# The order of key tiles, gates and the first merge stage ahead of attention A in layer 0

## The reference, cut to what matters

```python
qa = apply_rope(rms_norm(br['qa'], lw['q_norm']), cos, sin)      # 8 heads
ka = apply_rope(rms_norm(br['ka'], lw['k_norm']), cos, sin)      # 2 key/value heads
a_out = dense_gqa(qa, jnp.concatenate([ka, ka_ctx], axis=1),
                  jnp.concatenate([br['va'], va_ctx], axis=1), N_KV_A)
ya = (a_out * jax.nn.silu(br['ga'])) @ lw['w_proj_a']
g_a, g_b, g_c = jnp.split(jax.nn.sigmoid(h @ lw['w_gate'] + lw['b_gate']), N_BRANCH, axis=-1)
```

## Time and profile before

| | us |
|---|---|
| median of 3 runs | 1404.5 (1404.39 to 1404.72) |
| the profiled execution, its own time | 1406.98 |
| its span in the trace | 1405.2 |
| PE busy | 1361.3 (97%) |
| DVE busy | 768.6 (55%) |
| POOL busy | 692.9 (49%) |
| ACT busy | 624.2 (44%) |

### The profile page before, as it was taken

The page is one execution under the profiler, slowest core; times in us unless marked ns, Lnnn a source line. Parts: engine busy times, 40 slices in busy tenths (PEclk is TensorE's granted clock), DMA queues, the critical chain, the costliest instruction groups (busy, mean ns, idle before and its releaser), DMA issues.

```text
span 1405.2 us, 22465 instructions
## 1 busy us (share of the span) xinstructions
PE 1361.3 (97%) x8654; PEld 1259.1 (90%) x8654; DVE 768.6 (55%) x1605; ACT 624.2 (44%) x1298; POOL 692.9 (49%) x500
## 2 busy tenths in 40 slices
PE   7999999999999999999999999999999999999997
PEld 5898989899888899999888988998989989999985
DVE  5656773263884511656685577722468715036557
ACT  4336876334765221223264478851367633222230
POOL 3455565234565354355653566642256554445453
PEclk9999999999999999999999999999999999999999
DMA  9412101222112344354421211012121042225421
GB/s 362 137 61 65 31 31 33 74 79 68 39 46 68 127 151 150 112 204 136 135 97 47 87 61 31 31 46 79 61 63 43 31 136 68 68 76 195 131 80 75
DMA packets 36762, 126.94 MB, mean 90 GB/s; under 512 B 5040, under 2 KB 5680, under 8 KB 36656
## 3 DMA queue, kind: packets, MB, share of 16 engines
q1 hardware_dynamic: 29952, 108.54, 23.1%
q10 hardware_dynamic: 6704, 16.97, 3.4%
HBM read 119.73 MB, written 5.77 MB: 89 GB/s over the span
## 4 chain that ended last, share of the span: by engine, by line
PE 85%; DVE 5%; POOL 4%; ACT 2%; issue 2%; DVEq 0%; POOLq 0%; ACTq 0%
PE ps L949 50%; PE ps L897 6%; PE ps L899 6%; PE ps L898 6%; PE ps L1096 4%; PE ps L1086 3%; PE ps L1088 2%; PE ps L1107 2%; PE ps L1108 2%; POOL with_eps L1778 1%; POOL w_lo L1794 1%; DVE x L1759 1%; PE ps L966 1%; POOL p_f_a L1820 1%; PE ps L1115 1%
## 5 line engine op out<-in xcount | busy, mean ns | idle before, releaser
L1794 POOL TENSOR_TENSOR w_lo<-raw,w_hi 128x1024 fp32r<-128x1024 f32 x148 | 360.2, 2440 | 270.6 <-ACT w_hi L1151 184.9
L949 PE MATMUL ps<-h_hi,w_hi 128*128 128x320 f32 x1280 | 295.6, 312 | 8.7 <-DVE g_c L1699 4.6
L949 PE MATMUL ps<-h_hi,w_lo 128*128 128x320 f32 x1280 | 291.9, 309 | 0.0
L949 PE MATMUL ps<-h_lo,w_hi 128*128 128x320 f32 x1280 | 291.5, 309 | 0.0
L949 PEld LDWEIGHTS ps<-h_hi,w_hi 128*128 128x128 f32 x1280 | 218.1, 188 | 25.5 <-DVE g_c L1699 6.0
L1151 ACT ACTIVATE w_hi<-raw 128x1024 fp32r<-128x1024 f32 x148 | 154.1, 1055 | 148.3 <-DMA raw<-in_weights 70.6
L949 PEld LDWEIGHTS ps<-h_lo,w_hi 128*128 128x128 f32 x1280 | 215.2, 188 | 1.6
L949 PEld LDWEIGHTS ps<-h_hi,w_lo 128*128 128x128 f32 x1280 | 215.0, 188 | 1.8
L897 PE MATMUL ps<-w_hi,h_hi 128*128 128x512 f32 (+1 forms) x360 | 129.8, 361 | 1.2 <-POOL w_lo L1794 1.0
L899 PE MATMUL ps<-w_hi,h_lo 128*128 128x512 f32 (+1 forms) x360 | 128.3, 357 | 0.0
L898 PE MATMUL ps<-w_lo,h_hi 128*128 128x512 f32 (+1 forms) x360 | 128.0, 356 | 0.0
(11 more groups left out here) (184 smaller groups left out, 2630.3 us busy)
## 6 DMA issues: line engine op xcount, KB each, us to landing
raw<-in_weights SPq DMA_DIRECT2D x190, 512.0 KB, 3.4
raw_more<-in_weights SPq DMA_DIRECT2D x10, 512.0 KB, 10.4
x<-in_x_sample ACTq DMA_DIRECT2D x6, 512.0 KB, 9.8
x_mid<-x ACTq DMA_DIRECT2D x5, 512.0 KB, 2.6
x<-x_mid ACTq DMA_DIRECT2D x5, 512.0 KB, 6.7
y_sample<-x SPq DMA_DIRECT2D x3, 512.0 KB, 2.6
pack<-in_pack ACTq DMA_DIRECT2D x2, 528.0 KB, 6.7
x<-in_x_sample SPq DMA_DIRECT2D x2, 512.0 KB, 5.2
```

What stands on the lines that cost most here:

```text
L949: last = pe.matmul(ps[:, s + half, 0:HALF], w[:, u % RING, cols], acts[:, k, half * HALF:(half + 1) * HALF], start=k == 0 and part == 0, s ...
L1794: did(pool.tensor_tensor(w_lo[:, n % RING, :], raw_tile(r), w_hi[:, n % RING, :], ALU.subtract), w_ready)
```

## The change

In layer 0 the list between the key and value product and attention A is written anew. Before, the order is: key and value tiles 0 and 1; gate 2; queries 4; tile 2; zeros; gate 3; exponential table; queries 0; key tile 0; tile 3; key tile 1; tile 4; key tile 2; merge stage 0 whole; key tile 3; cached keys; 2 warm matmuls; key tile 4.

After, it is: tile 0; cached keys; tile 1; zeros; gate 2; queries 4; key tiles 0 and 1; tiles 2 and 3; gate 3; key tile 2; tile 4; exponential table; queries 0; key tile 3; first half of merge stage 0; key tile 4; second half. The two warm matmuls are left out.

The state outputs move from the event of the cached tile to that of key tile 1, in both layers and for both branches.

```diff
     if l == 0:
         kvm = mm("kv_a")
+        first_z = ("z", l, 0, 0)
+        first_z_of = chunks(first_z, 2)
         out.extend([qs[1], qs[2], *whole(gate("a", 0)), queries[1], qs[3], *whole(gate("a", 1)), queries[2], qs[4],
-                    kvm[0], queries[3], qs[0], kvm[1], kv[0], kv[1], *whole(gate("a", 2)), queries[4], kv[2],
-                    ("zeros", l), *whole(gate("a", 3)), ("table_of_exp", l, "a"), queries[0], keys[0], kv[3], keys[1], kv[4], keys[2], *whole(("z", l, 0, 0)), ("pool", 0, 1, 2, 3, 4, 5),
-                    keys[3], keys[5], ("warm", 2, 4), keys[4]])
+                    kvm[0], queries[3], qs[0], kvm[1], kv[0], keys[5], kv[1], ("zeros", l), *whole(gate("a", 2)), queries[4],
+                    keys[0], keys[1], kv[2], kv[3], *whole(gate("a", 3)), keys[2], kv[4], ("table_of_exp", l, "a"), queries[0],
+                    keys[3], first_z_of[0], keys[4], first_z_of[1], first_z, ("pool", 0, 1, 2, 3, 4, 5)])
...
                         if t == CACHE:
                             did(act.activation(vv[:, CACHE, :, 0, :], cache_v[:, "ab".index(br), :, :], ACT.Copy), v_hi_made)
+                        if t == 1:
                             act.wait_ge(staged, NO[("in", l, "kv_" + br, 0)] + 1)
                             load(state_out, outs[f"state_{br}_k"][0, l], k_st[:, 0, :, 0, :])
                             load(state_out, outs[f"state_{br}_v"][0, l].rearrange("p h d -> p (h d)"), v_st[:, :])
```

## The result

The changed kernel took 1407.68 us (median of 11 executions, 1405.21 to 1408.75), the kernel before 1404.39 (11 executions, 1403.49 to 1405.84). The two medians are 3.3 us apart. The ratio estimated from all these executions is 1.0019, that is 2.7 us, with a 95% interval of 1.0011 to 1.0027: 1.5 to 3.8 us slower, small but clear of 1. All executions of this study together give medians of 1406.4 (24 of the changed kernel) and 1404.5 (76 of before): **1.9 us slower**. The forecast was 0.6 us slower, 1405.1 us, and the range ended at 1407.4: the first median lies 0.3 us above that end, the second and the pooled one within the range.

A forecast was written before the change was run, and what follows sets the result against it. PE was taken to bound the kernel (85% of the chain that ended last). The terms +4.2 + 1.5 - 3.6 - 1.5 + 0 gave +0.6 us on the median of 1404.5: 1405.1 us, range 1403.2 to 1407.4.

The forecast's parts named there:

- Step 1: Ahead of the third gate: PE waits for DVE to drain the cached keys' bank; gate starts 4.2 us later.
- Step 2: At the third gate: the clock falls within or after the stall, costing 1.5 us (bounds 0.4 and 3.0).
- My sign for a wrong size: Around the third gate: the low clock lasting beyond one stretch would make the prediction's size wrong.
- Step 3: From the third gate's Silu to the scores: 3.6 us less than 21.4, mainly from waits that go.
- Step 4: At the first scores: with the waits gone the clock stays up, 1.5 us less (bounds 0 and 1.5).
- Step 5: State outputs moved on ACT in four lead-ins: no effect, 0, bounds -0.5 and +0.5 us for all four.
- A: Rival: no stall at the third gate, sum -4.9, 1399.6 us; chance 0.08.
- B: Rival: the clock dip at the scores stays, sum +2.1, 1406.6 us; chance 0.12.
- C: Rival: the clock stays low through the third gate, sum +6.1, 1410.6 us; chance 0.07.
- D: Rival: waits return at key tile 4 or first probabilities, 1 to 2 us lost, 1406 to 1407 us; chance 0.10.

The follow-up runs named there:

- e1: The changed kernel with layer 0's cached keys transposed into PSUM bank 0 instead of bank 5: 1399.97 us against 1404.76 before.
- e6: The changed kernel with the cached keys moved between the third and fourth gate, no bank fixed by hand: 1405.52 us against 1404.16 before.
- e7: The changed kernel, unedited, profiled a second time to look at its clock: 1405.81 us.
- e8: The changed kernel, unedited, profiled a third time to look at its clock: 1405.1 us.
- e9: The changed kernel, unedited, timed again against the kernel before: median 1406.14 us against 1404.49, ratio 1.0011.
- e10: The changed kernel with 8 instead of 3 warm matmuls in PE's wait at 24 us: 1405.66 us against 1404.49 before.
- e2: The changed kernel with 16 unneeded warm matmuls between the cached transposes and the third gate: 1403.96 us, ratio to before 0.9993.
- e5: The kernel before with more warm matmuls (7 and 8 instead of 2 and 2) in its two waits ahead of the scores: 1403.36 us against 1404.16.
- e11: The changed kernel with the cached keys in bank 0 and 8 instead of 3 warm matmuls at 24 us: 1399.76 us against 1404.49 before.
- e3: The kernel before with only the state outputs moved to key tile 1, both layers and branches: 1404.75 us against 1404.76.
- e4: The kernel before with only the cached keys moved ahead of the third gate, state outputs with key tile 1: 1409.1 us against 1404.76.

## Why the prediction was right, and where its sizes were off

**Step 1, the stall: right, in place, cause and size.** 4.0 us from the transposes to the gate against 4.2, and 3.62 idle against 3.9 (just under the 3.7 to 4.1 that I had named as its sign). The short duration of the last instruction held: 0.28 us. e1 shows that the bank is the cause and not the place in the list, and in e6 the wait follows the bank to the next gate.

**Step 2, the clock on the third gate: right that it falls, too small.** I took the 1.5 us of another dip. The profiles show 9.47 - 7.04 = 2.4 at first, then 2.5 and 1.4 (e7, e8), and 1.6 in e9 and in e10. The gate in e10 (102.98 - 94.30 = 8.68):

```profile
94.30 0.80 PE L951 MATMUL ps<-h_hi,w_hi 128*128 128x320 f32 x2 [3.61 <-DVE vv L1621]
...
102.98 0.60 PE L1065 MATMUL ps<-ident_r,q_st 128*128 128x128 f32 x4
```

As times, the median of e10 (stall empty) less the usual time of e2 (stall filled; 7 of its 11 executions lie at 1403.7 to 1404.0) gives 1405.66 - 1403.93 = 1.7. All lie between my bounds of 0.4 and 3.0. My sign for a wrong size, a low clock beyond one stretch, did come in the first profile: about 4.9 us of the gate's work ran at the low level (twice the 2.43 lost), against 3.3 us in the dip at the scores.

**Step 3, the lead from gate to scores: right.** 122.98 less the Silu at 105.45 (gate end at 105.25 plus the 0.2 of the earlier trace rows) is 17.5, by the trace's record of that start; 17.8 was worked out, 21.4 was before. Most of the 0.3 too much is the warm matmuls, which I took at their duration of 0.6; the scores start 0.37 behind them (122.61 to 122.98). The steps kept apart by a tenth did fit: key tile 4 came at 117.97, and no wait stands there. Where no execution has a low clock the kernels are cleanest to compare: e2 is at 1403.9 (7 of 11), and e5, the kernel before without its dip, at 1403.1 to 1403.4 (6 of 11), say 1403.2: +0.7 for a sum of +4.2 - 3.6 = +0.6. By the traces it is +0.3: 28.9 us from the cached transposes to the first scores in e2 (90.27 to 119.17), 28.6 from the gate to the scores in before (92.43 to 121.05). e11 is at 1399.8, -3.4 for 0.2 - 3.6 = -3.4.

**Step 4, the dip at the scores: gone, as forecast, but credited too highly.** The term was taken from one execution of before and subtracted from the median. That execution took 1406.98, and 74 of the 76 timed ones were faster. It had two low stretches and the later start. e3's profile, at 1404.4, had one, and by their times a quarter of the executions of before (19 of 76) probably had none. Against the executions without any, the median of before carries 1404.5 - 1403.2 = 1.3 us of low clock altogether. Even where the dip is there it isn't worth 1.5 us. From the first scores to the start of the last matmul PE takes 1273.7 us in before (121.05 to 1394.79) and 1273.6 in e3, but 1272.5 in e5 and 1272.6 in the changed kernel: the dip costs 1.1 to 1.2 us. The 3.30 - 1.82 counted what the dip takes at its own place, and some of that must come back later. So the mis-sized term of the sum is the -1.5; e5 gives -0.8 between medians, and -1.3 is the most that the times allow. And one reading went wrong: I compared the span with the median, found 0.7 us, and left it at that, instead of comparing the execution's own 1406.98 with the 1404.5. That difference of 2.5 us was the sign that this profile was no usual execution.

**Step 5, state outputs: right**, 0 (e3).

**The sum anew**, as differences between medians and groups: +0.7 (stall and lead) + 1.7 (low clock on the gate) less 0.8 to 1.3 (dip at the scores) is +1.1 to +1.6 us, where +0.6 was forecast. These terms come from the same times as the total, so that they add up is no test of them; the gate's own length in the profiles is one, with 1.6 us in e10 for the 1.7. e10 itself, without the early low stretch, is 1.2 us slower than before. The changed kernel as it stands is 1.7 (e9) to 1.9 us (pooled) slower, 0.5 to 0.8 more than e10. The early low stretch, which both kernels have in some executions and to which the prediction gave no term, is the likely reason. The changed kernel's times spread over one range, and the stretch raises their median; before's fall into groups (19 at or below 1404.0, 40 from 1404.1 to 1405.0, 17 above 1405.7), and the median stays in the middle one. Of the first measurement's 3.3 us, 1.4 are more than the pooled 1.9; in that session 6 of 11 executions of the changed kernel were above 1407.6, later 2 of 13. Whether chance alone made that share isn't settled. The prediction wasn't right by luck: its two large terms, +4.2 and -3.6, held singly to 0.3 us, and both clock terms were off to the same, slow side.

**Rivals.** A was the price of the way not taken: 1399.6 was worked out for a kernel without the stall, and e1 has 1399.97. B didn't happen: the changed kernel showed 1.00 at its scores in all four profiles. C didn't happen: the low level ended within the gate in the same four and in that of e10, though in the first it lasted longer than the 3.3 us on which I had counted. D didn't either, the waits didn't return.

## What to carry to other kernels

An allocator that walks the schedule turns a harmless early placement into a dependence: before moving a step forward, find out which buffer it gets, who takes that buffer next, and when its slowest user, here the vector engine's queue behind a split on GpSimd, lets it go. The same order with one bank fixed by hand (e1) went from 1.9 us slower to 4.8 us faster. And take a clock dip that a single profile shows as a matter of chance: compare that execution's own time with the median before counting its dip as gain or loss.

## What the runs showed of the hardware that I had not expected

The granted clock falls after short idle spots, but not each time. The idle spot of 1.1 to 1.2 us at 24 us was followed by a clock of 0.50 in five profiles (before, the changed kernel at first, e4, e5, e6) and by 1.00 in six (e1, e2, e3, e7, e8, e9). A wait of 1.45 us ahead of key tile 4 in e4 was followed by no fall, nor were the 3.15 us of e6; 3.6 us were followed by a low stretch in every one of the profiles (the changed kernel's four, e4, e10). The length of the loss varies as well, 1.4 to 2.5 us behind the same 3.6 us. The rule of the Trainium skill on idle gaps ("TensorE: Matmul & The Clock Gate", section "Why this matters for your kernels") names a limit above the idle spots behind which the clock fell at 24 us and at the scores; the traces decide against it as a safe limit. In e2 a 128-column matmul stood every 0.12 us in the place of the 3.6 us of idle time, and the level stayed at 1.00.
